# Residual phases of a float32r transformer kernel: high and low halves of an activation side by side, one 512-column matmul for both

## The reference

```
first_block:  h = h + 0.5 * swiglu(rms_norm(h), ffn1_w_in, ffn1_w_out)      # 2816 hidden
              h = h + token_mixer(rms_norm(h), ...)   # two attentions, gates, @ w_out
              h = h + 0.5 * swiglu(rms_norm(h), ffn2_w_in, ffn2_w_out)      # 2816 hidden
second_block: h = h + head_group_mixer(rmsnorm(h), ...)  # conv + retention, @ w_out
              h = h + memory_cross_attention(rmsnorm(h), mem_n, ...)        # @ xo_w
              h = h + square(relu(rmsnorm(h) @ up_w)) @ down_w              # 4096 hidden
              return rmsnorm(h)
```

## Time and profile before

| what | value |
|---|---|
| median of 3 executions | 1059.12 us |
| span of the profiled execution, first to last instruction | 1056.1 us |
| PE (matmul) busy | 1019.6 us, 97% |
| PEld (weight load) busy | 982.2 us, 93% |
| DVE (VectorE) busy | 688.7 us, 65% |
| ACT (ScalarE) busy | 508.4 us, 48% |
| mean granted TensorE clock | 0.991 |
| HBM read | 170.72 MB |

### The profile page before, as it was taken

How to read it: one execution, slowest core, us unless ns; L and a number is a source line. 1 busy time by engine, 2 the same in 40 slices (tenths; PEclk the granted TensorE clock), 3 DMA queues, 4 the chain that set the end, 5 groups by cost and what they waited for, 6 DMA issues and landing times.

```text
span 1056.1 us, 21171 instructions
## 1 busy us (share of the span) xinstructions
PE 1019.6 (97%) x8000; PEld 982.2 (93%) x8000; DVE 688.7 (65%) x1252; ACT 508.4 (48%) x832; POOL 31.1 (3%) x49
## 2 busy tenths in 40 slices
PE   4999999999999999999999999999999999999996
PEld 4999999989987789999999999887899999999996
DVE  4666664555676548776666548979666378885543
ACT  5544453363455545655444448341664365543431
POOL 4200000010100000000000000000000000000000
PEclk8999999999999999999999999999999999999998
DMA  6445465437732224655556456313454255556551
GB/s 218 160 178 172 167 230 178 150 118 237 239 120 92 90 80 141 200 193 185 180 200 232 166 184 214 120 61 120 165 174 141 100 180 183 191 184 199 169 189 42
DMA packets 46544, 172.71 MB, mean 164 GB/s; under 512 B 5498, under 2 KB 7682, under 8 KB 45968
## 3 DMA queue, kind: packets, MB, share of 16 engines
q1 hardware_dynamic: 44160, 162.58, 45.1%
q0 software_dynamic: 1360, 8.57, 2.5%
q10 hardware_dynamic: 960, 0.67, 0.2%
HBM read 170.72 MB, written 3.77 MB: 165 GB/s over the span
## 4 chain that ended last, share of the span: by engine, by line
PE 87%; DVE 7%; ACT 3%; issue 2%; DMA 1%; DVEq 0%; ACTq 0%
PE bank L384 26%; PE bank L386 25%; PE bank L385 25%; DVE cy L1291 3%; DVE wlo L365 1%; ACT whi L354 1%; PE bank L396 1%; PE bank L1089 1%; PE bank L779 1%; PE bank L781 1%; DMA res<-in_res 1%; PE bank L1474 1%; PE bank L1451 1%; PE bank L753 1%; PE bank L752 1%
## 5 line engine op out<-in xcount | busy, mean ns | idle before, releaser
L384 PE MATMUL bank<-xhi,whi 128*128 128x256 f32 (+1 forms) x1464 | 423.3, 289 | 10.9 <-DVE wlo L365 10.2
L386 PE MATMUL bank<-xhi,wlo 128*128 128x256 f32 (+1 forms) x1464 | 416.4, 284 | 0.0
L385 PE MATMUL bank<-xlo,whi 128*128 128x256 f32 (+1 forms) x1464 | 415.4, 284 | 0.0
L365 DVE TENSOR_TENSOR wlo<-raw,whi 128x1024 fp32r<-128x1024 f32 (+1 forms) x287 | 362.9, 1266 | 24.1 <-ACT whi L354 23.8
L354 ACT ACTIVATE whi<-raw 128x1024 fp32r<-128x1024 f32 (+1 forms) x287 | 311.5, 1086 | 129.6 <-PE bank L386 110.8
L384 PEld LDWEIGHTS bank<-xhi,whi 128*128 128x128 f32 x1464 | 277.4, 189 | 18.4 <-issue 17.5
L385 PEld LDWEIGHTS bank<-xlo,whi 128*128 128x128 f32 x1464 | 277.7, 190 | 0.2
L386 PEld LDWEIGHTS bank<-xhi,wlo 128*128 128x128 f32 x1464 | 277.4, 189 | 0.0
L384 PE MATMUL bank<-hid_hi,whi 128*128 128x256 f32 (+1 forms) x608 | 172.9, 284 | 0.0
L385 PE MATMUL bank<-hid_lo,whi 128*128 128x256 f32 (+1 forms) x608 | 172.6, 284 | 0.0
L386 PE MATMUL bank<-hid_hi,wlo 128*128 128x256 f32 (+1 forms) x608 | 171.8, 283 | 0.0
(11 more groups left out here) (258 smaller groups left out, 1163.5 us busy)
## 6 DMA issues: line engine op xcount, KB each, us to landing
raw<-in_w_f1in SPq DMA_DIRECT2D x44, 512.0 KB, 3.5
raw<-in_w_f2in SPq DMA_DIRECT2D x44, 512.0 KB, 3.5
raw<-in_w_mix SPq DMA_DIRECT2D x35, 512.0 KB, 3.5
raw<-in_w_up SPq DMA_DIRECT2D x32, 512.0 KB, 3.6
raw<-in_w_down SPq DMA_DIRECT2D x32, 512.0 KB, 4.1
raw<-in_w_f1out SPq DMA_DIRECT2D x16, 704.0 KB, 4.1
raw<-in_w_f2out SPq DMA_DIRECT2D x16, 704.0 KB, 4.2
raw<-in_w_mixb SPq DMA_DIRECT2D x20, 512.0 KB, 3.5
```

Of the source, the lines that this page charges most:

```text
L365: nc.vector.tensor_tensor(wlo[:, s, 0:tiles * P], raw[:, s, 0:tiles * P], whi[:, s, 0:tiles * P], ALU.subtract).then_inc(w_lo, 1)
L384: nc.tensor.matmul(out, whi[:, s, w], rhs_hi(t), start=start and t == 0, stop=False)
L385: nc.tensor.matmul(out, whi[:, s, w], rhs_lo(t), start=False, stop=False)
L386: mm = nc.tensor.matmul(out, wlo[:, s, w], rhs_hi(t), start=False, stop=stop and t == tiles - 1)
```

## The change

In the five residual phases that are 256 columns wide, the high and the low part of an activation tile lie side by side in one buffer, [high 256 | low 256]. One matmul of high weights by these 512 columns replaces L384 and L385 and fills a whole PSUM bank: high product in columns 0 to 255, low product in 256 to 511. The third matmul (low weights by high activation, 256 columns) adds to the first half. VectorE then adds the two halves to `res` one after the other, the second waiting for the first by a new semaphore `res_half`. `f1out` (272 columns) and all phases that aren't residual keep three matmuls per tile; only the layout of their activations changes.

```
-        xhi = place("xhi", [P, KT, W2], F32R)
-        xlo = place("xlo", [P, KT, W2], F32R)
+        x2 = place("x2", [P, KT, 2, W2], F32R)
-        hid_hi = place("hid_hi", [P, F2T * NX], F32R, at)
-        hid_lo = place("hid_lo", [P, F2T * NX], F32R, at)
+        hid2 = place("hid2", [P, 2 * F2T * NX], F32R, at)
...
-        oy_hi = place("oy_hi", [P, 16, NX], F32R, at)
-        oy_lo = place("oy_lo", [P, 16, NX], F32R, at)
+        oy2 = place("oy2", [P, 16, 2, NX], F32R, at)
...
-        oz_hi = place("oz_hi", [P, 8, NX], F32R, at)
-        oz_lo = place("oz_lo", [P, 8, NX], F32R, at)
-        mem_hi = place("mem_hi", [P, KT, NX], F32R, at)
-        mem_lo = place("mem_lo", [P, KT, NX], F32R, at)
+        oz2 = place("oz2", [P, 8, 2, NX], F32R, at)
+        mem2 = place("mem2", [P, KT, 2, NX], F32R, at)
...
+        res_half = sem("res_half")
...
-                nc.tensor.matmul(out, whi[:, s, w], rhs_hi(t), start=start and t == 0, stop=False)
-                nc.tensor.matmul(out, whi[:, s, w], rhs_lo(t), start=False, stop=False)
-                mm = nc.tensor.matmul(out, wlo[:, s, w], rhs_hi(t), start=False, stop=stop and t == tiles - 1)
+                hi, lo, both = rhs(t)
+                first, last = start and t == 0, stop and t == tiles - 1
+                if both is None:
+                    nc.tensor.matmul(out, whi[:, s, w], hi, start=first, stop=False)
+                    nc.tensor.matmul(out, whi[:, s, w], lo, start=False, stop=False)
+                    mm = nc.tensor.matmul(out, wlo[:, s, w], hi, start=False, stop=last)
+                else:
+                    nc.tensor.matmul(out, whi[:, s, w], both, start=first, stop=False)
+                    mm = nc.tensor.matmul(out[:, 0:NX], wlo[:, s, w], hi, start=False, stop=last)
...
+        halves = {"wo": 0, "f2out": KT, "wo2": 2 * KT, "xo": 3 * KT, "down": 4 * KT}
...
-                    outs.append(start_group(pe, g0, mpb, 0, j)[:, 0:width])
+                    outs.append(start_group(pe, g0, mpb, 0, j)[:, 0:T if width == T else 2 * NX])
...
-                        nc.vector.scalar_tensor_tensor(res_tile(k, full), flat_or_two(out, full), scale,
-                                                       res_tile(k, full), ALU.mult, ALU.add).then_inc(acc_free, 1)
+                        if full:
+                            nc.vector.scalar_tensor_tensor(res_tile(k, full), flat_or_two(out, full), scale,
+                                                           res_tile(k, full), ALU.mult, ALU.add).then_inc(acc_free, 1)
+                        else:
+                            nc.vector.scalar_tensor_tensor(res_tile(k, full), two(out[:, 0:NX]), scale,
+                                                           res_tile(k, full), ALU.mult, ALU.add).then_inc(res_half, 1)
+                            dve.wait_ge(res_half, k + (halves[name] + 1))
+                            nc.vector.scalar_tensor_tensor(res_tile(k, full), two(out[:, NX:2 * NX]), scale,
+                                                           res_tile(k, full), ALU.mult, ALU.add).then_inc(acc_free, 1)
...
-        ffn_rhs = {w: (lambda t, w=w: (hid(hid_hi, t, w), hid(hid_lo, t, w))) for w in (T, NX)}
+        ffn_rhs = {T: lambda t: (hid(0, t, T), hid(1, t, T), None), NX: lambda t: (hid(0, t, NX), None, hid_both(t))}
```

More of the change, by code:

```diff
@@ L309, in res_tile, with x_tile @@
             return res[:, m, 0:T] if full else seg(res[:, m, :])
-        def x_tile(t, m, full):
-            return t[:, m, 0:T] if full else two(t[:, m, 0:NX])
+        def x_tile(low, m, full):
+            return x2[:, m, low, 0:T] if full else two(x2[:, m, low, 0:NX])
         def flat_or_two(ap, full):
@@ L319, in gain, with hid, hid_both @@
             return gains[:, n * KT + m:n * KT + m + 1] if isinstance(m, int) else gains[:, bass.ds(m + n * KT, 1)]
-        def hid(t, j, n):
-            return t[:, 0:FT * T].rearrange("p (j t) -> p j t", t=n)[:, j, :] if n == T else \
-                t[:, 0:F2T * NX].rearrange("p (j t) -> p j t", t=n)[:, j, :]
+        def hid(low, j, n):
+            count = FT if n == T else F2T
+            return hid2[:, 0:2 * count * n].rearrange("p (j s t) -> p j s t", s=2, t=n)[:, j, low, :]
+        def hid_both(j):
+            return hid2[:, 2 * j * NX:2 * (j + 1) * NX]
         def bodies(eng, n, per, body):
@@ L375, in start_group, with strip @@
             return ps[banks[g0 + (per if not isinstance(i, int) else per * i) + j]]
-        def strip(out, s, tiles, rhs_hi, rhs_lo, start=True, stop=True, at=0, before=None, begin=0, end=None):
+        def strip(out, s, tiles, rhs, start=True, stop=True, at=0, before=None, begin=0, end=None):
             for t in range(begin, tiles if end is None else end):
@@ L441, in act_x @@
         def act_x(n, m, full):
-            nc.scalar.activation(x_tile(xhi, m, full), res_tile(m, full), ACT.Copy, scale=gain(n, m)).then_inc(x_hi, 1)
+            nc.scalar.activation(x_tile(0, m, full), res_tile(m, full), ACT.Copy, scale=gain(n, m)).then_inc(x_hi, 1)
         def act_square(n, m, full, par):
@@ L526, in body @@
                         act.wait_ge(f["prod"], u + 1)
-                        nc.scalar.activation(hid(hid_hi, u, width), hd[:, 0:width], ACT.Copy).then_inc(f["hhi"], 1)
+                        nc.scalar.activation(hid(0, u, width), hd[:, 0:width], ACT.Copy).then_inc(f["hhi"], 1)
             bodies(act, counts[name], 4, body)
@@ L535, in hidden_lo @@
                 dve.wait_ge(f["hhi"], u + 1)
-                nc.vector.tensor_tensor(hid(hid_lo, u, width), hd[:, 0:width], hid(hid_hi, u, width),
+                nc.vector.tensor_tensor(hid(1, u, width), hd[:, 0:width], hid(0, u, width),
                                         ALU.subtract).then_inc(f["hlo"], 1)
@@ L574, in one @@
                 q = j % cpm
-                return strip(out, (c0 + j) % RING, tiles, lambda t: rhs(q * tiles + t)[0],
-                             lambda t: rhs(q * tiles + t)[1], start=q == 0, stop=q == cpm - 1, **part)
+                return strip(out, (c0 + j) % RING, tiles, lambda t: rhs(q * tiles + t), start=q == 0,
+                             stop=q == cpm - 1, **part)
             def head():
@@ L1082, in pe_mixb @@
                 if q < 20:
-                    hi, lo = x_rhs("packed")
-                    mm = strip(out[:, 0:NX], s, KT, hi, lo, before=wait_x(pe, N_MIXB) if q == 0 else None)
+                    rhs = x_rhs("packed")
+                    mm = strip(out[:, 0:NX], s, KT, rhs, before=wait_x(pe, N_MIXB) if q == 0 else None)
                 else:
@@ L1590, in body @@
                     act.wait_ge(up_prod, 4 * i + j + 1)
-                    nc.scalar.activation(hid(hid_hi, 4 * i + j, NX), hd[:, 0:NX], ACT.Copy).then_inc(up_hhi, 1)
+                    nc.scalar.activation(hid(0, 4 * i + j, NX), hd[:, 0:NX], ACT.Copy).then_inc(up_hhi, 1)
             bodies(act, F2T, 4, body)
@@ L1596, in low @@
                 dve.wait_ge(up_hhi, u + 1)
-                nc.vector.tensor_tensor(hid(hid_lo, u, NX), hd[:, 0:NX], hid(hid_hi, u, NX), ALU.subtract).then_inc(up_hlo, 1)
+                nc.vector.tensor_tensor(hid(1, u, NX), hd[:, 0:NX], hid(0, u, NX), ALU.subtract).then_inc(up_hlo, 1)
             def body(i, edge):
```

67 lines of the change are left out of this document (35 added, 32 removed).

## The result

The changed kernel takes 1053.5 us in the median of 9 runs (1049.41 to 1057.32); the kernel before, beside it, 1059.14 (9 runs, 1057.30 to 1062.92). The ratio is 0.9943, with a 95% interval of 0.9926 to 0.9961. A second comparison (e11) gave 1051.24 against 1059.85, 0.9927 [0.9908, 0.9945]. So the change makes the kernel faster, by 5.6 and by 8.6 us (0.6 and 0.8%), where the forecast was 7.8. The profiled execution has a span of 1051.7 us and a time of 1053.5; before, the span was 1056.1 beside a median of 1059.12.

The account below looks back on a forecast made before the run. TensorE's rate of issue was taken as the bound. Matmuls -8.7, short phases -1.1, kernel end +0.45 and layout +1.5 made -7.8 us, so 1051.3 us against the median of 1059.12; range 1046 to 1059.5.

Parts of the forecast that it names:

- Matmuls in `f2out` and `down`: In `f2out` and `down`, 432 tiles each save 20.2 ns by one matmul and weight load fewer: -8.7 us.
- my ends (213.3 and 240): Bracket in ns for the 512-column matmul: array time alone and the slowest plain float32 row; 219 was taken.
- My remark that the excess did not grow with the columns: TensorE's cost beyond column time: 12.9 ns at 256 columns, 11.5 at 272, so fewer, wider matmuls can be faster.
- The rule of the Trainium skill that I weighed: Isolated matmul gap is column time plus 2.5 ns, making the removed instructions of `f2out` and `down` worth 1.1 us.
- Rival 1: Weight loads hold TensorE's rate; two per tile give 320 ns in `f2out` and `down`, -16.0 us, 1043.2 us; chance 0.12.
- Rival 2: Excess belongs to float32r columns, the instruction costs only 2.7 ns; +1.0 us in all, 1060.1 us; chance 0.08.
- Rival 3: 512-column matmul takes 240 ns or more in each `f2out` and `down` tile; slower, 1061.3 us at 240; chance 0.08.
- rival 4: VectorE's pair of adds costs 0.8 us instead of 0.45 in `wo`, `wo2`, `xo`; 1058.9 us; chance 0.07.
- The second add in `wo`, `wo2`, `xo`: VectorE, at 2.65 us per tile, sets the pace there; +0.2, -0.9 and -0.4 us, together -1.1.
- The end of the kernel: After `down`, nothing hides the second add in the chain of add, square and `sqsum`: +0.45 us.
- The layout: In `f2in`, `mixb`, `xq`, `up`, two of three x matmuls slow instead of half, 118.1 ns on average: +1.5 us.
- The time outside the span: The 3.0 us around the profiled span, between 1056.1 and the median of 1059.12, taken to stay.

Follow-up runs that it names:

- e11: The changed kernel once more, unchanged, timed beside the kernel before: 1051.24 us against 1059.85, ratio 0.9927.
- e9: Changed kernel with other widths: `down` 384 + 128 columns, then 256; `f2out` both matmuls 512 wide; 1086.07 us in one run.
- e4: Changed kernel without the second add in `wo`, `wo2`, `xo` (low-part product missing from the sum): 1050.52 us, ratio 0.9922 to the kernel before.
- e10: Changed kernel with x parts 320 words apart instead of 288, `hid` parts 288 instead of 256: 1059.32 us against 1058.77, ratio 1.0010.
- e1: Changed kernel's layout alone, with three 256-column matmuls and one add everywhere: 1055.09 us against 1059.43 for the kernel before, ratio 0.9969.
- e12: The layout alone run again, three matmuls and one add: 1053.84 us against 1059.85 for the kernel before, ratio 0.9951.
- e6: Kernel before with only x laid out in high and low pairs: 1057.24 us, ratio 0.9971 to the kernel before.
- e2: Changed kernel with the 512-column matmul and second add only in `f2out` and `down`: 1053.83 us, ratio 0.9958 to the kernel before.
- e3: Changed kernel with the 512-column matmul and second add only in `wo`, `wo2`, `xo`: 1056.85 us, ratio 0.9979 to the kernel before.
- e8: Changed kernel with GpSimd instead of VectorE adding the squares to their sum in `wo`, `wo2`, `xo`: 1057.63 us, ratio 0.9973 to the kernel before.

## Why the prediction was right, and where it was not

The time, 1053.5 against 1051.3, lies in the range, and the sign holds. Of the mechanism, that TensorE's rate is the bound and that fewer, wider matmuls raise it holds, at half the size; that the number came so near is luck. By the traces the sum of -7.8 us was made of one term twice too large, one of the wrong sign, one too large and one right:

- *Matmuls in `f2out` and `down`, forecast -8.7.* They gave 1.75 + 2.56 = 4.3 us, 10 ns per tile and not 20.2. The step that failed is the price of the 512-column float32r matmul: I took 219 ns from the plain float32 ones of the earlier trace rows; it is 230. The neighbour at 256 columns is 120, as I left it. A plain matmul with as much array time did not stand for a wide float32r one; 230 was inside my ends (213.3 and 240). My remark that the excess did not grow with the columns, from 256 against 272, was wrong too: over 512 columns it is 16.7 ns where 256 have 13. The rule of the Trainium skill that I weighed (TensorE: Matmul & The Clock Gate, Back-to-back issue gap), given there for an isolated matmul, would have made the removed instruction worth 2.5 ns and the gain 1.1 us; the trace does not agree, with 10 ns and 4.3 us.
- *Rival 1, the weight load.* A tile of 320 ns, with loads off the bound, did not come: the loads' share in `down` fell to 76.92 of 88 and the tile stayed at 350. The load looks like the bound at 128 columns (110 ns, e9), not at 256. *Rival 2* named a part of it: of the 512-column matmul's excess about 7 ns go with the columns and 10 with the instruction. *Rival 3* (240 or more) and *rival 4* (0.8 for the pair) are refuted by 230 ns and by the next rows.
- *The second add in `wo`, `wo2`, `xo`, forecast -1.1.* The mechanism stands to the letter. One tile of VectorE in `wo`, to be set against the earlier trace rows:
```profile
427.01 0.42 DVE L646 SCALAR_TENSOR_TENSOR res<-bank,res 128x256 f32<-128x256 f32 x1
427.47 0.42 DVE L649 SCALAR_TENSOR_TENSOR res<-bank,res 128x256 f32<-128x256 f32 x1
427.81 1.22 DVE L364 TENSOR_TENSOR wlo<-raw,whi 128x1024 fp32r<-128x1024 f32 x1
428.94 0.48 DVE L467 SCALAR_TENSOR_TENSOR x<-res,gains,x 128x256 fp32r<-128x256 f32 x1
429.34 0.42 DVE L462 TENSOR_TENSOR sqsum<-sqsum,sq 128x256 f32<-128x256 f32 x1
429.67 0.42 DVE L646 SCALAR_TENSOR_TENSOR res<-bank,res 128x256 f32<-128x256 f32 x1
```
429.67 - 427.01 = 2.66 us (forecast 2.65), the pair 0.46 apart (0.45), nothing idle. At the end of `wo`, answering to the earlier trace rows, the last add and TensorE's eighth tile:
```profile
440.30 0.42 DVE L646 SCALAR_TENSOR_TENSOR res<-bank,res 128x256 f32<-128x256 f32 x1
```
```profile
442.29 0.39 PE L386 MATMUL bank<-x,whi 128*128 128x256 f32 x1 [0.57 <-DVE x L467]
```
From the first add (422.04) to the last are 18.26 us (forecast 18.21), from there to the eighth tile 1.99 (1.98). The wait costs `f2in` 0.85 us and `up` 0.62, where I said some 1 us. Set against the layout kernel, by phases, `wo` with `f2in` is +0.4 us, `wo2` with `xq` -0.6, `xo` with `up` 0.0: -0.2 together. This is 1.6 us gained in the phases (e4, without the waits) less 1.47 for the waits. Part of the shortfall follows from the first term: `wo2` and `xo` start their last stretch 4 and 14 tiles of 10 ns sooner, not of 20. The rest, some 0.1 us per phase, I did not trace.
- *The end of the kernel, forecast +0.45.* 1042.45 - 1041.09 = 1.36 us against 0.90 in the earlier trace rows: +0.46.
```profile
1041.09 0.42 DVE L646 SCALAR_TENSOR_TENSOR res<-bank,res 128x256 f32<-128x256 f32 x1 [7.66 <-PE bank L391]
1041.55 0.42 DVE L649 SCALAR_TENSOR_TENSOR res<-bank,res 128x256 f32<-128x256 f32 x1
1042.45 0.43 DVE L462 TENSOR_TENSOR sqsum<-sqsum,sq 128x256 f32<-128x256 f32 x1 [0.48 <-ACT sq L452]
```
- *The layout, forecast +1.5.* Wrong sign. The step that failed is the reading that two thirds of the x matmuls would be slow: `f2in` and `up` kept their pace, 117.8 ns. Half of that reading was right. In `f2in` before, the tiles of x on the multiples take 359.0 ns from start to start and the others 348.3 (means over 29 chunks of the trace), that is 119.7 and 116.1 per matmul, where I had 119.6 and 115.2. But with the high part on the multiples and the low one off, a tile takes 353.4, midway, and not the 355.5 of two slow matmuls and one fast; a part's place does not set the time of its own matmul alone. "The multiples that hid always has" was wrong: `hid` starts 24 words off them (e10). What changed lies where I had costed nothing: `f1in` about -1.1 us, the gates of `mix` -0.5, the branch before `wo` -0.35, `f1out`, `mixb` and `xq` -0.1 to -0.2 each, about -2.3 in the traces of the layout kernels. The medians of runs say more, 4.3 and 6.0 (e1, e12), but those runs also had the higher mean clock (0.9917 and 0.9927, against 0.9902 of the kernel before); at one clock it is 2.5 to 3.3, and e6, with the same clock on both sides, has 3.1. Whether the layout has a part in the clock is open.
- *The time outside the span, 3.0 us.* I added it as a thing that stays. In every execution since, time and span lie 1.8 to 1.9 us apart; the other 1.2 us are then most likely that the profiled execution lay below its kernel's median. As the same median was the base of the forecast, the difference of -7.8 is not touched.

With the measured terms the sum is -4.3 - 0.2 + 0.45 - 2.3 = -6.4 us, between the 5.6 and 8.6 of the two comparisons, whose runs of the changed kernel had a mean clock of 0.989 and 0.992. The forecast came near by luck, because a gain taken twice too large stood beside a gain taken for a loss. Shown by experiments are the pair's worth in the long phases (e2, by phases), that the second adds take back most of what the short phases gain (e3, e4), and that the layout of x alone is faster (e1, e6, e12). Not shown is why: e10 shows that the place of the parts sets the pace of `f2in`, which the layout had left as it was; in `f1in` its 125.3 ns lie between the 124.4 and the 125.9 that the changed kernel itself had in two traces.

## What to carry to other kernels

Merging two matmuls on the same weights into one of 512 columns was worth 10 ns per merge here, on a tile of 360; take the price of a wide matmul from one of the same number format, and where there is none, keep the whole bracket in the sum. Where the product ends in a read-modify-write, the merge costs another operation per output tile, and in phases with one output tile per chunk it turns VectorE into the bound: merge only where a tile has several chunks, and look at the first wait in the phase behind. Run the layout by itself before the gain is put down to the arithmetic.

## What the runs showed of the hardware

- From 256 columns up a float32r matmul with its own weight load cost about 10 ns and 0.43 ns per column on `hid` (120, 177, 230 ns for 256, 384, 512); one of 128 columns cost 110 ns, if its neighbour kept 120, near the 105 of a one-column matmul with its load. Splitting 512 into 384 + 128 made the tile 57 ns longer.
- The place of the moving operand matters by 2%: `f2in` ran at 117.8 ns from start to start and, with its parts on multiples of 64 words from the start of x, at 120.0. Beside that, the pace of one program in `f1in` differed by 1.2% between two executions (125.9 and 124.4 ns) at the whole clock.
- GpSimd's addition of 256 columns took 0.80 us and doubled VectorE's operation beside it, 0.48 to 0.97.
- After TensorE had waited 1.24 us behind `wo` and 1.23 behind `xo`, its granted clock fell 2.0 and 1.4 us later (e8); after waits of 0.57 and 0.35 in the same places of the changed kernel it did not.
- The granted clock fell now and then at the head of `f1in` and in `mix` (0.83 in 260 to 280 us of the changed kernel, 1.00 before), and with it `mix` lay between 168.5 and 173.7 us over fourteen traces; among the runs of the kernel before, the time fell from 1061.40 to 1058.23 us as the mean clock rose from 0.989 to 0.992, about 1 us for 0.001.
